# A recurrent pass cut into three steps of one group each, its late levels run one step later and its state walk two steps behind

## What is computed

```
def step(S, inp):
    r_t, w_t, k_t, v_t, a_t, b_t = inp
    sa = jnp.einsum('bhij,bhj->bhi', S, a_t)
    S = S * w_t[:, :, None, :] + sa[..., None] * b_t[:, :, None, :] + v_t[..., None] * k_t[:, :, None, :]
    return S, jnp.einsum('bhij,bhj->bhi', S, r_t)
```

## Time and profile before

| | |
|---|---|
| median of three runs | 2550.72 us |
| the profiled execution | 2552.2 us, its span 2549.9 us |
| TensorE busy | 87% of the span |
| VectorE, ScalarE, GpSimd busy | 55%, 32%, 47% |
| mean granted TensorE clock | 0.925 |

### The profile page before, as it was taken

One profiled execution on the slowest core, in us unless ns is written; L12 is line 12 of the kernel. 1 busy time (PEld: TensorE's weight loads), 2 busy tenths in 40 slices (PEclk: granted clock), 3 DMA queues, 4 the chain that ended last, 5 costly groups with the idle time before them and its releaser, 6 DMA issues.

```text
span 2549.9 us, 56210 instructions
## 1 busy us (share of the span) xinstructions
PE 2213.5 (87%) x22038; PEld 1868.7 (73%) x22038; DVE 1401.9 (55%) x2028; ACT 824.4 (32%) x2139; POOL 1207.3 (47%) x708
## 2 busy tenths in 40 slices
PE   6799999988888989886867999999894999798876
PEld 4699989877777878775867976777694776565555
DVE  6766666666666566664445413445415172638655
ACT  1532233325545555453212222333201111211331
POOL 1366656633223132233855831222384897775134
PEclk8899999999988889896987999999897999899998
DMA  2233344372333233323211221000022221221001
GB/s 86 85 141 141 153 150 151 136 196 44 81 62 71 58 71 74 69 48 109 79 64 50 83 74 34 33 33 23 27 83 94 74 91 42 66 83 58 17 0 66
DMA packets 158904, 197.54 MB, mean 77 GB/s; under 512 B 120992, under 2 KB 123296, under 8 KB 156448
## 3 DMA queue, kind: packets, MB, share of 16 engines
q1 hardware_dynamic: 158752, 195.25, 25.2%
HBM read 156.24 MB, written 38.99 MB: 77 GB/s over the span
## 4 chain that ended last, share of the span: by engine, by line
PE 56%; DVE 11%; issue 5%; ACT 4%; POOL 1%; DVEq 1%; ACTq 0%; POOLq 0%
PE wide L797 9%; PE wide L1224 8%; PE wide L1225 8%; PE wide L1226 8%; PE wide L1701 4%; PE wide L1810 2%; PE wide L812 2%; PE wide L820 1%; PE wide L1586 1%; PE wide L1766 1%; DVE x_w L1022 1%; PE wide L814 1%; DVE b_and_k L1015 1%; PE wide L1794 1%; PE wide L2063 1%
## 5 line engine op out<-in xcount | busy, mean ns | idle before, releaser
L1077 POOL TENSOR_TENSOR n_levels<-n,masks 128x192 f32<-128x192 f32 (+1 forms) x96 | 117.8, 1239 | 437.5 <-ACT n L958 437.5
L1224 PE MATMUL wide<-mixed_high,w_high_rwkv_in 128*128 128x264 f32 x720 | 213.0, 296 | 27.8 <-ACT log_decay L435 18.9
L1226 PE MATMUL wide<-mixed_high,w_low_rwkv_in 128*128 128x264 f32 x720 | 207.5, 288 | 0.0
L1341 DVE TENSOR_TENSOR sq_sum<-sq_sum,squares 128x528 f32<-128x528 f32 (+1 forms) x54 | 87.3, 1617 | 178.6 <-ACT squares L1306 178.6
L1225 PE MATMUL wide<-u_low_second,w_high 128*128 128x512 f32 x464 | 185.5, 400 | 0.0
L1248 POOL TENSOR_TENSOR w_high<-weights,con 128x1024 fp32r<-128x1024 f32 x60 | 147.5, 2459 | 73.6 <-PE wide L1226 63.7
L355 PE MATMUL wide<-mixed_in,weights 128*128 128x264 f32 x672 | 158.7, 394 | 13.7 <-DVE mixed_in L325 12.3
L1224 PEld LDWEIGHTS wide<-mixed_high,w_high_rwkv_in 128*128 128x128 f32 x720 | 139.0, 193 | 36.2 <-ACT log_decay L435 25.1
L1251 POOL TENSOR_TENSOR w_low<-weights,w_high 128x1024 fp32r<-128x1024 f32 x60 | 157.6, 2627 | 4.7
L355 PEld LDWEIGHTS wide<-mixed_in,weights 128*128 128x128 f32 x672 | 128.9, 193 | 41.0 <-issue 9.5
L797 PE MATMUL wide<-x_w,n_levels 64*64 64x64 f32 x2752 | 121.8, 231 | 37.8 <-DVE x_w L1022 21.0
(11 more groups left out here) (325 smaller groups left out, 6495.0 us busy)
## 6 DMA issues: line engine op xcount, KB each, us to landing
weights<-in_stream SPq DMA_DIRECT2D x200, 512.0 KB, 3.3
forms<-form SPq DMA_DIRECT2D x16, 2020.5 KB, 6.3
forms_in<-forms SPq DMA_DIRECT2D x96, 144.0 KB, 4.5
forms_in<-forms SPq DMA_DIRECT2D x32, 288.0 KB, 4.5
gate_bonus<-forms SPq DMA_DIRECT2D x16, 576.0 KB, 4.0
r_ahat_r<-forms SPq DMA_DIRECT2D x32, 144.0 KB, 3.1
mixed<-gate_bonus SPq DMA_DIRECT2D x14, 264.0 KB, 2.1
gated<-mixed SPq DMA_DIRECT2D x14, 264.0 KB, 4.8
```

The costliest lines, as they stand in the source:

```text
L1077: return pool.tensor_tensor(n_lvl[:, first:last, grp(g), :], n_all[:, grp(g), :].unsqueeze(1).to_broadcast([P, n, GC, C]), b_con[:, 1 + fi ...
L1224: pe.matmul(dst, w[0], x[0], start=start, stop=False)
L1226: return pe.matmul(dst, w[1], x[0], start=False, stop=stop)
```

## The change

The three groups no longer run side by side. One list of a step, `steps`, replaces `schedule` and `merged`. A pass is three steps, one for each group g. In its step a group goes through G (two chunks, `G pair`, then one, `G last`), N, W, M, E and XW of level 0 and E of level 1. XW of level 1 and all later levels and A run in the step of the next group. The walk is two steps behind: in the step of group 0 it takes group 1 of the pair before, in that of group 1 its group 2, in that of group 2 the same pair's group 0. `post` of pair i-2 is in the step of group 0; `centre`, `square` and `norm` of pair i-1 are in that of group 2.

`start` on VectorE goes. W's first value is now a product of x (which GpSimd has made) with the unit tile on TensorE, copied by ScalarE. A moves from `odd_bank` to the group's `inv_bank`. The semaphores of E and XW are split into early and late ones, and some semaphores of the first stage serve again. GpSimd makes all levels of a group in one go, x first.

```diff
+        def steps(i):
+            def there(back):
+                return not isinstance(i, int) or 0 <= i - back < PAIRS
+            out = []
+            for g in range(GROUPS):
+                walk_back, walk_g = ((1, 1), (1, 2), (0, 0))[g]
+                last_back, last_g = (0, g - 1) if g else (1, GROUPS - 1)
+                def new(name):
+                    return [(name, 0, g)] if there(0) else []
+                def old(name, lv):
+                    return [(name, last_back, (lv, last_g))] if there(last_back) else []
+                def walk(n):
+                    return [("walk", walk_back, (GC * walk_g + n // 2, n % 2))] if there(walk_back) else []
+                def first(name):
+                    return [(name, 0, (int(name[-1]), g))] if there(0) else []
+                def done(name, arg=0):
+                    if name == "post":
+                        return [(name, 2, arg)] if g == 0 and there(2) else []
+                    return [(name, 1, arg)] if g == GROUPS - 1 and there(1) else []
+                out += new("G pair") + old("XW", 1) + walk(0) + new("N") + old("E", 2) + new("G last") + walk(1) + old("XW", 2) + done("centre")
+                out += done("post", 0) + walk(2) + old("E", 3) + new("W") + walk(3) + done("square") + old("XW", 3) + new("M") + done("norm")
+                out += [("E", *item[1:]) for item in first("E0")] + walk(4) + old("E", 4) + [("XW", *item[1:]) for item in first("XW0")]
+                out += done("post", 1) + old("XW", 4) + [("E", *item[1:]) for item in first("E1")] + walk(5)
+                out += [("A", back, arg[1]) for _, back, arg in old("A", 0)]
+            return out
...
+                elif item in ("G pair", "G last"):
+                    n = GROUPS * k + arg
+                    if item == "G pair":
...
+                        if n > 1:
+                            pe.wait_ge(q["a_rows"], n - 1)
+                        if n > 0:
+                            pe.wait_ge(q["b_k_made"], 4 * n)
+                    else:
+                        pe.wait_ge(q["b_k_made"], 4 * n + 2)
...
+                elif item == "W":
+                    n = GROUPS * k + arg
+                    pe.wait_ge(q["x_start"], 2 * n + 2)
+                    pe.wait_ge(q["v_rows"], 2 * n + 2)
+                    if arg == 0 and k > 1:
+                        pe.wait_ge(Y_ACT.sem, Y_ACT.at(k - 2, 3))
+                    group(odd_bank[1], of(x), lambda c: eye[:], grp(arg), w_mm)
...
+                elif item == "W":
+                    wait_heads(act, w_mm, W_MADE + GROUPS * k + arg + 1)
+                    act.activation(xw[:, W_OF + par, flat(arg)], odd_bank[1][:, 0:GC * C], ACT.Copy).then_inc(q["w_start"], 1)
...
-                elif item == "start":
-                    dve.wait_ge(q["b_k_made"], B_K * i + b_k_done(arg))
-                    for hd, rows in enumerate(HEAD_ROWS):
-                        dve.tensor_tensor(xw[rows, W_OF + par_, flat(arg)].rearrange("p (c n) -> p c n", c=GC), b_k[rows, par_, hd, grp(arg), 0, :],
-                                          eye[rows].unsqueeze(1).to_broadcast([C, GC, C]), ALU.add).then_inc(q["w_start"], 1)
...
             for g in range(GROUPS):
-                pool.wait_ge(q["n_rows"], 2 * (GROUPS * i + g + 1))
-                levelled(g, 0, 1)
...
+                pool.wait_ge(q["n_rows"], 2 * n + 2)
                 x = xw[:, X_OF + par_, flat(g)].rearrange("p (c n) -> p c n", c=GC)
                 pool.tensor_tensor(x, n_all[:, grp(g), :], over_chunks(b_con[:, 0, :]), ALU.mult).then_inc(q["x_start"], 1)
-                pool.wait_ge(q["x_start"], 6 * i + 2 * g + 1)
+                pool.wait_ge(q["x_start"], 2 * n + 1)
                 pool.tensor_tensor(x, x, over_chunks(eye[:]), ALU.add).then_inc(q["x_start"], 1)
-            for g in range(GROUPS):
-                levelled(g, 1, LEVELS)
+                if not (isinstance(i, int) and n < GROUPS):
+                    wait_heads(pool, late_e_mm, 3 * n - 6)
+                levelled(0, 1)
+                levelled(1, LEVELS)
```

More of the change, by code:

```diff
@@ L729, in wait_scan @@
         def wait_scan(eng, pair, parity):
-            eng.wait_ge(scan_loaded[parity], turn_of(pair, parity, SCAN_DMAS))
+            eng.wait_ge(scan_loaded[parity], X_DMA + turn_of(pair, parity, SCAN_DMAS))
         def wait_gate(eng, pair, parity):
[L735 to L766, removed]
-                    for g in range(GROUPS):
[L768 to L774, removed]
+            eng.wait_ge(gate_loaded[parity], X_DMA + turn_of(pair, parity, 16))
@@ L776, in program @@
         HALVES = (slice(0, 5), slice(5, NC))
         Y_DVE, Y_ACT = Count(q["y_dve"], 6), Count(q["y_act"], 4)
[L778 to L794, removed]
+        STATES = NC - 1
@@ L796, in by_head, with pe_pass, group, of @@
+        def pe_pass(pe, i, par_):
+            def by_head(out, lhsT, rhs, done=None):
                 for hd, rows in enumerate(HEAD_ROWS):
-                    mm = pe.matmul(out[rows], lhsT[rows], rhs[rows], start=start, stop=stop)
+                    mm = pe.matmul(out[rows], lhsT[rows], rhs[rows], start=True, stop=True)
                     if done:
                         mm.then_inc(done[hd], 1)
-            def walk(c, part):
-                block = slice(0, C)
+            def group(out, lhsT, rhs, chunks, done):
+                chunks = range(NC)[chunks]
+                for n, c in enumerate(chunks):
+                    by_head(out[:, n * C:(n + 1) * C], lhsT(c), rhs(c), done if n == len(chunks) - 1 else None)
+            def of(ap):
+                return lambda c: ap[:, c * C:(c + 1) * C]
+            def walk(p, pw, c, part):
+                block, n = slice(0, C), GROUPS * p + c // GC
@@ L855, in pe_pass @@
                 elif item == "N":
[L856 to L861, removed]
+                    n = GROUPS * k + arg
+                    if n > 0:
+                        pe.wait_ge(q["m_rows"], n)
+                        pe.wait_ge(q["w_start"], n)
@@ L862, in pe_pass @@
+                    if arg == 1 and k > 1:
+                        pe.wait_ge(Y_ACT.sem, Y_ACT.at(k - 2, 4))
+                    for at, c in enumerate(range(NC)[grp(arg)]):
+                        upper, lower = (b_f[rows, par, c] for rows in HEAD_ROWS)
                         a_v = (upper[:, A_AT:V_UPPER + 1, :], lower[:, V_LOWER:A_AT + 1, :])
@@ L929, in pe_pass, with act_pass @@
                                 mm.then_inc(y_turned[hd], 1)
[L931 to L944 removed]
+        def act_pass(act, i, par_):
```

327 lines of the change are left out of this document (160 added, 167 removed).

## The result

The changed kernel takes 2650.55 us (median of 4 runs, 2641.11 to 2661.5) against 2551.76 us for the kernel before in the same comparison (2550.43 to 2553.3): ratio 1.0388, interval 1.0348 to 1.0429. It is slower by 99 us where 50 were forecast, and 0.55 us above the upper end of the range. Its runs spread over 20 us, those of before over 3.

A forecast was written before the change was run, and what follows sets the result against it. TensorE, busy 88% of passes 1 to 15, was taken as the bound. Profiled 2552.2 us + 44.6 (layout with fill) - 1.6 (drain) + 7 (clock) = 2602.2, the median 1.5 lower: 2600.7 us; range 2530 to 2650.

The forecast's parts named there:

- Layout: Recurrent stage, first G to last A: a pass 41.8 us against 39.7, the whole 673.1 against 628.5, +44.6 us.
- the 0.55 ahead of XW2: Plain step: TensorE idle 0.55 us before XW2, since ScalarE's E2 copy is queued behind N's four copies.
- E0's copy: Step with `norm`: ScalarE's root with its table load holds this copy, so XW0 starts at 10.7 in place of 9.8.
- E4: E product of level 4, old group, on TensorE: in a plain step XW3 to XW0, with it, run closed up, to 10.5.
- ScalarE's table load of 1.28 us: Step with `norm`: comes with ScalarE's root, once in two passes, and holds the E0 copy.
- Clock: TensorE in the passes: 0 to 3.5 us a pass lost to the lower clock; 0.5 taken, +7 us.
- the tail of the `post` step: 12.6 to 15.0 us with one A in it: looks like the old head of the pass, where the clock fell.
- the clock stays low: Rival: clock falls at two of three step ends, about 4.5 us a pass lost, 2660 us; chance 0.14.
- Fill: First three steps of the recurrent stage, 9.5, 12.0 and 13.2 us: 34.7 us against 33.0.
- Drain: Behind the last A: some 20 us less walk is covered by GpSimd's splitting, 0; TensorE's two `z_low` waits go, -1.6 us.
- Collisions: VectorE's second `centre` instruction, in the step of group 2, waits 0.6 us for GpSimd's level product.
- The value of W by a product: Removes `start`, 5.6 us of VectorE a pass, and TensorE's wait on it; costs TensorE 0.35 us a group.

The follow-up runs named there:

- warm: Changed kernel with 48 unused records on TensorE ahead of A's wait and 20 behind A, in the `post` step alone: 2606.97 us, ratio 1.0199.
- pool3: GpSimd splits three stored pairs in place of six: in the kernel before 2553.33 us (ratio 0.998), in `reordered` 2507.44 us (ratio 0.981).
- start_back: Changed kernel with W's product undone, VectorE's addition back at the same place of the list: 2645.98 us, ratio 1.0344.
- gate_behind: Changed kernel with two items swapped in the `post` step, the last XW's add ahead of VectorE's gate instructions: 2586.07 us, ratio 1.0117.
- w_alone: Kernel before, groups side by side, with only W as a product and ScalarE copy, GpSimd making x first: 2508.04 us, ratio 0.9802.
- reordered: Changed kernel, list order only: XW1 before G pair, v copies behind E2's, `square` behind XW3, `norm` and `post` 1 behind last XW, walk before E1: 2524.22 us.

## Why the prediction was right in sign and wrong in size

- **Layout**, forecast +44.6 us: right in size. The step with `post` is 15.03 to 15.08 us (15.0 forecast), with `norm` 14.04 (14.1), pass 1 40.7 (40.2). The step of group 1 is 12.8 where the clock holds (12.7), so a pass would be 41.9 (41.8). Part of this is luck. Within the `norm` step errors cancel: the 0.55 ahead of XW2 is 0.15, and what holds XW0 is not E0's copy but E4, which waits 0.66 for XW3's add (the row at 754.80). The forecast also put ScalarE's table load of 1.28 us into this step; in the kernel before it stood there in seven passes, in the changed kernel only in pass 1, whose `norm` step is 14.45 us.
- **Clock**, forecast +7, bounds 0 to 3.5 us a pass: this is the step that failed. Steps behind `post` are 3.5 us too long, 49 us over fourteen passes, at the upper bound that the prediction had written down itself. The place was right, "the tail of the `post` step (12.6 to 15.0 with one A in it)", and so were the rows compared with it; taken was a value "near the low end" since no idle piece is over 1.5 us. That reason was no reason: the pieces before the fall are 0.54, 0.96 and 0.52 us. The rival "the clock stays low" came near to the mechanism, at 2660, but had it fall at two of three step ends, and it fell at one (but for the one long `norm` step, of which `warm` has one too).
- **Fill**, forecast 34.7 us: 37.7 (543.95 to 581.68), with the clock at 0.76 in it; before it was 0.85 in about the same window. From first G to last A the change cost 98.1 us (99.0 less 0.9), where 51.6 were forecast (44.6 and 7). The 46.5 us between them are the clock with 42 (49 less 7), the fill with 3.0, the one long `norm` step with 1.5 and layout and pass 1 with about 2, less about 2 by which the last two steps came out shorter than laid out.
- **Drain**, forecast 0 and -1.6: the out projection starts 46.6 us behind SP's loads, as against 44.2 before, and behind it the profiled run wins back 3.9 (101.4 less 97.5), where 1.6 were forecast. What the shorter drain saves did not come through, as forecast; the `pool3` pair shows the cover to be GpSimd.
- **Collisions**, 0.6 us in `centre`: real but smaller. Its median is 1123 ns where it was 759, 0.36 us more. The gate instructions were not hit, at 0.71 each. The victim that had not been named is `state_decayed` (L1012): 1.68 to 1.76 us in nine of 112, where 254 ns is its median, each in a step that the clock had already made late, with 7.3 us of TensorE's time behind them and in three of the nine a second fall of the clock. Besides `centre`, the prediction had looked for victims only among the gate instructions and `norm`'s product. The Trainium skill (GPSIMD Engine Reference, 1. Specifications) names VectorE instructions in a two-port mode beside those with two SBUF inputs, and this one has one tensor input; whether it ran in a two-port mode no row shows.
- **The value of W by a product** was right as the prediction had it (the wait on `start` goes), but 5.6 us of VectorE and a wait of 18.6 were set against the new latencies and never priced alone. Alone it is worth 50 us in the old order and 0.47 us a pass in the new one, where TensorE stands on VectorE's addition for 0.3 us at most (`start_back`).

So the 99 us are 49 behind the `post` step, by the clock and what follows from it, and 50 of layout and fill, and W's gain of the old order is not there to set against them. That the clock's part comes from the gate ahead of the add is shown by `gate_behind` and `warm` together. What makes the clock fall by such different amounts behind the same tail, in two passes of fourteen hardly or not at all, is in part the second fall behind the collision; the rest is open and was not tried. Nor is a thin tail enough: the `norm` step ends with idle pieces of 0.66, 0.63 and 0.56 us, and the `post` step behind it is 15.03 to 15.08 us every time.

## What to carry to other kernels

Where an in-order engine has slack work and a link of the critical chain in its list, put the link first: the swap of two items gave back 64 of 99 us. Do not price a thin tail by its longest idle piece; if the same profile shows that the clock fell behind such a tail, charge the whole loss, and try a version with matmuls that nobody uses in the gap, which tells clock from layout in one run. And try the parts of a combined change alone: here the small one was the good one.

## What the runs showed of the hardware that was not expected

- The clock fell to 1.2 GHz behind a tail whose longest idle piece was 0.96 us, at 1.04 us busy in 2 (682 to 684), and a step of the same instructions then took 12.8 to 19.5 us. The Trainium skill (TensorE: Matmul & The Clock Gate, "A second HAM failure mode: psum-queue depth-cycling") tells of a kernel whose clock swings between its two levels because TensorE idles briefly and often between groups of matmuls; the rows agree with that, and give its price, 3.5 us a pass on average.
- Work for nothing can pay: 68 records that nobody uses in a step of 15.04 us made it 0.37 us longer and the next 3.5 us shorter on average.
- A fallen clock brings a collision that is not there at full clock: it moves VectorE's `state_decayed` under GpSimd's level product (1.76 us for 0.25), TensorE stands for up to 1.35 us behind it, and in three of nine such steps the clock, already back at 1.00, falls again.
- Runs of a kernel that is on the edge of this spread over 8 to 20 us (the changed kernel, `start_back`), while `gate_behind` and `warm` stay within about 4 and `w_alone` within 1. The spread alone proves nothing: `reordered`, with a clock of 1.00 in its window, has 8.
